# Attention stage of a hybrid decoder layer: later joins of first halves, later sample parts, and products with values ahead of the transposes

## The chip, the core and the metric

The kernel runs on one core of one Trainium2 chip. The metric is device time in microseconds (us) of one launch, median of several runs. A core has five engines with instruction streams of their own: TensorE (PE) multiplies matrices, VectorE (DVE) and ScalarE (ACT) do elementwise work and reductions, GpSimd (POOL) elementwise work, SyncE (SP) issues the transfers here. Streams meet at semaphores. PE writes its results to banks of PSUM, from which DVE and ACT read.

## What is computed

One layer for a prompt of 2048 rows and 8 samples of 8 rows, which share weights: a normalised, modulated input goes through one wide projection; branch A is sliding-window attention in three groups of 8 heads with strides 1, 4 and 16; branch B a gated recurrence; both are projected, gated, merged and added to the input. The part that the change touches is branch A:

```python
s = q @ k.T * scale - slope * dist          # per head, block of 128 queries: own and previous key block
m = max(s); p = exp(s - m); l = sum(p)
o = (p @ v) / l;  lse = m + log(l)
...
alpha = softmax over the 3 groups of lse     # head slot j of the three groups
o_a = sum over groups of alpha * o           # then times silu(z_A)
```

Samples do the same against a cache of earlier keys and values.

## The kernel before

Stages run one after the other: the input stage, `phase_weave` (projections and recurrence), `phase_mix` (attention), `phase_tail` (merge and output projection). The change is in `phase_mix`.

**Jobs and steps.** `JOBS` are the 12 combinations of 4 head pairs and 3 groups (2, 1, 0 in each pair); a job has 16 blocks of 128 queries, a step each, so N = 192. Steps of group 2 (and every fourth of group 1, the first of group 0) see one key block, those of the rest two; the text calls them light and full. Light steps fill steps 0 to 15, 48 to 63, 96 to 111 and 144 to 159.

**One block through the engines.** `score` (PE, L1482) multiplies queries with keys; `largest` (DVE, L1696) adds the distances and takes the minimum of the negated scores; `weights` (ACT, L1613) takes exponentials; `turn` (PE, L1490) transposes them; `copy_turned` (ACT, L1621) copies the transposes out of PSUM; `weigh` (PE, L1503) multiplies them with the values and a column of ones; `leave_sums` (DVE, L1703) moves the result to `o_out`, and SP stores it to `sums` in DRAM (L1392), four blocks at a time. At step n, PE runs `score(n)`, `turn(n-1)`, `weigh(n-2)`; ACT `weights(n)`, then `copy_turned(n-1)`; DVE `leave_sums(n-3)`, then `largest(n)`.

**Sample parts.** The samples' attention is cut into 4 groups (two samples each) of 13 parts, placed between steps by `at(i, k)`: parts 0 to 3 are scores (L1521, L1527), 4 to 7 transposes (L1539), 8 to 11 products with cached values (L1554), 12 selects the output (L1570). At a step that has a part, PE runs it behind `weigh`. The tables `S_PREPARE` (queries, DVE), `S_LARGEST`, `S_EXP`, `S_COPY`, `S_LOAD` (SP) and so on follow from `at`. SP loads the 32 stages of cached keys (L1402) and values (L1406) two ahead, each behind the part that frees its buffer; a stage is 2 MB but for the fourth of each four, which is smaller.

**Joins.** When a pair has its three groups, their rows are joined in two halves of 8 blocks. SP loads the rows from `sums` (L1425, 1.6 MB) and the gates (L1426); DVE takes the least maximum (`join_least`, L1756), ACT exponentials, DVE the weights (`join_weight`); POOL makes the weighted sums (DVE in the last pair); PE transposes each block (`join_turn`, L1590); DVE multiplies with the gate; SP stores. `start(jp, half)` and the tables `J_LOAD`, `J_LEAST`, `J_EXP`, `J_WEIGHT`, `J_SUM`, `J_TURN` place these. For the first halves of pairs 0 to 2, J_LOAD is at step 53, 101 or 149 and J_LEAST two steps later. Every table is read in a loop over n that each engine runs in order.

**Loads of a job.** At the fifth step of a job SP loads queries, keys, distances and values of the next (L1370 to L1380, 3.4 MB), behind the last use of the buffers, which is the end of the job before.

Of the kernel before, what the change touches and what calls it, by code (L numbers as in the profile page):

```python
# [21 lines left out]
PAIRS = 4  # L22
# [1225 lines left out]
def phase_mix(nc, t, dr):  # L1248
# [4 lines left out]
    N = len(JOBS) * BLK  # L1253
# [4 lines left out]


    SPAN, PARTS = 46, 13  # L1260
    at = lambda i, k: 4 + SPAN * i + k * SPAN // PARTS
    S_PE = {at(i, k): (i, k) for i in range(SB // 2) for k in range(PARTS)}
    S_PREPARE = {at(i, 0) - 2: i for i in range(SB // 2)}
    S_LARGEST = {at(i, c) + 1: (i, c) for i in range(SB // 2) for c in range(4)}
# [7 lines left out]

    start = lambda jp, half: BLK * (3 * jp + 3) + (5 + 20 * half if jp < PAIRS - 1 else 8 * half - 3)
    J_HALVES = [(jp, half) for jp in range(PAIRS) for half in range(2)]
    turn_at = lambda jp, half: start(jp, half) + (12 if jp < PAIRS - 1 else 6 + 2 * half)
    J_LOAD = {start(*x): x for x in J_HALVES}
    J_LEAST = {start(*x) + 2: x for x in J_HALVES}
    J_EXP = {start(*x) + 3: x for x in J_HALVES}
    J_WEIGHT = {start(*x) + 4: x for x in J_HALVES}
    J_SUM = {start(*x) + (7 if x == (PAIRS - 1, 1) else 5): x for x in J_HALVES}  # L1280
    S_LAST = [at(i, PARTS - 1) for i in range(SB // 2)]

    def turn_slot(jp, half, b):
# [12 lines left out]
    with ExitStack() as ctx:  # L1296
# [65 lines left out]
        with nc.Block() as block:  # L1362
# [107 lines left out]
            def _(pe):  # L1470
                def score(n):
                    a, i = divmod(n, BLK)
                    first = first_of(n)
                    if i == 0:
                        pe.wait_ge(q_in[a % 2], 16 * (a // 2 + 1))
                        pe.wait_ge(k_in[a % 2], 16 * (a // 2 + 1))
                    if n:
                        pe.wait_ge(max_done, 2 * n)
                    for h in range(2):
                        q = q_sb[a % 2][h * HD:(h + 1) * HD, i * P:(i + 1) * P]  # L1480
                        k = k_sb[a % 2][h * HD:(h + 1) * HD, (i - 1 + first) * P:(i + 1) * P]
                        pe.matmul(s_ps[h][:, first * P:], q, k, start=True, stop=True).then_inc(s_done, 1)  # L1482

                def turn(n):
                    pe.wait_ge(exp_done, 2 * n + 2)
                    if n >= 2:
                        pe.wait_ge(copy_done, n - 1)
                    for h in range(2):
                        for b in range(first_of(n), 2):
                            mm = pe.transpose(t_ps[n % 2][:, 2 * h + b, :], probs[n % 2][:, h, b * P:(b + 1) * P], t["ident"][:, :])  # L1490
                    mm.then_inc(t_done, 1)

                def weigh(n):
                    a, i = divmod(n, BLK)
                    first = first_of(n)
                    if i == 0:
                        pe.wait_ge(v_in[a % 2], 64 * (a // 2 + 1))
                    pe.wait_ge(copy_done, n + 1)
                    if n:
                        pe.wait_ge(o_done, n)  # L1500
                    for h in range(2):
                        for b in range(first, 2):
                            mm = pe.matmul(o_ps[:, h, :], probsT[n % 2][:, 2 * h + b, :], v_sb[a % 2][:, i + b - 1, h, :],  # L1503
                                           start=(b == first), stop=(b == 1))
                    mm.then_inc(pv_done, 1)
# [67 lines left out]
                def sample_part(i, k):  # L1573
                    if k < 4:
                        sample_scores(i, k)
                    elif k < 8:
                        sample_turn(i, k - 4)
                    elif k < 12:
                        sample_weigh(i, k - 8)
                    else:  # L1580
                        sample_out(i)

                def join_turn(jp, half, b):
                    nth = NTH[jp, half]
                    pe.wait_ge(sums, 5 * (nth + 1))
                    if nth or b:
                        pe.wait_ge(jx_done, HB * nth + b)
                    if samples_ahead(turn_slot(jp, half, b)):
                        pe.wait_ge(so_done, samples_ahead(turn_slot(jp, half, b)))
                    pe.transpose(jt_ps[:, :], joined[:, b].rearrange("p h d -> p (h d)"), t["ident"][:, :]).then_inc(jt_done, 1)  # L1590

                for n in range(END):
                    if n < N:
                        score(n)
                    if 1 <= n <= N:
                        turn(n - 1)
                    if 2 <= n <= N + 1:
                        weigh(n - 2)
                    if n in S_PE:
                        sample_part(*S_PE[n])  # L1600
                    if n in J_TURN:
                        join_turn(*J_TURN[n])

            @block.scalar
            def _(act):
# [24 lines left out]
                def sample_copy(i, r):  # L1630
                    act.wait_ge(st_done, 4 * i + r + 1)
                    if i and r == 0:
                        act.wait_ge(stage_done, 8 * i)
                    src = x_ps[:, :].rearrange("p (m q) -> p m q", q=P)
                    if r < 3:
                        act.copy(s_probsT[:, 4 * r:4 * r + 4, :], src[:, :, :]).then_inc(s_copy_done, 1)
                        return
                    act.copy(s_probsT[:, 12:13, :], src[:, 0:1, :])
                    act.copy(s_probsT[0:G * ST, KEYS, :], src[0:G * ST, 1, :]).then_inc(s_copy_done, 1)

                def join_weights(jp, half):
                    act.wait_ge(diff_done, NTH[jp, half] + 1)
                    act.activation(wgt[:, :, :, :], wgt[:, :, :, :], ACT.Exp).then_inc(e_done, 1)

                act.preload_act_table_set("natural_log_exp_and_others")
                for n in range(END):
# [6 lines left out]
                    if n in S_COPY:  # L1653
                        sample_copy(*S_COPY[n])
                    if n in J_EXP:
                        join_weights(*J_EXP[n])

# [24 lines left out]
            def _(dve):  # L1682
# [61 lines left out]
                def sample_leave(i):  # L1744
                    new = slice(2 * i * ST, 2 * (i + 1) * ST)
                    dve.wait_ge(ot_done, i + 1)
                    dve.wait_ge(zs_in, 16)
                    dve.tensor_tensor(o_s[:, :, new], ot_ps[:, :, :], z_s[:, :, new], ALU.mult).then_inc(so_done, 1)

                def join_least(jp, half):  # L1750
                    nth = NTH[jp, half]
                    dve.wait_ge(rows_in, 48 * (nth + 1))
                    if nth:
                        dve.wait_ge(sums, 5 * nth)
                    neg_max = rows[:, :, :, :, HD + 1]
                    dve.tensor_tensor(j_least[:, :, :], neg_max[:, 0], neg_max[:, 1], ALU.min).then_inc(small, 1)  # L1756
                    dve.wait_ge(small, 7 * nth + 1)
                    dve.tensor_tensor(j_least[:, :, :], j_least[:, :, :], neg_max[:, 2], ALU.min).then_inc(small, 1)
                    dve.wait_ge(small, 7 * nth + 2)
                    dve.tensor_tensor(wgt[:, :, :, :], j_least[:, :, :].unsqueeze(1).broadcast_to([P, G, HB, 2]), neg_max,  # L1760
                                      ALU.subtract).then_inc(diff_done, 1)
# [29 lines left out]
                for n in range(END):  # L1791
# [12 lines left out]
                    if n in S_OUT:  # L1804
                        sample_leave(S_OUT[n])
                    if n in J_LEAST:
                        join_least(*J_LEAST[n])
                    if n in J_WEIGHT:
                        join_weight(*J_WEIGHT[n])
                    if n in J_SUM and J_SUM[n][0] == PAIRS - 1:  # L1810
                        weighted_sums(dve, *J_SUM[n])
                    if n - 1 in J_TURN:
# [408 lines left out]
```

## Time and profile before

| | us |
|---|---|
| median of 3 runs (3141.14 to 3145.24) | 3144.12 |
| profiled execution, own time | 3146.13 |
| its span | 3144.3 |
| PE busy over the span | 2896.0 (92%) |
| DVE, ACT, POOL busy | 1322.7, 1077.5, 820.1 |
| granted clock of PE, mean of the span | 0.941 |

In the profile, PE is a matmul and PEld the load of its stationary operand; the granted clock is 1.00 at 2.4 GHz and 0.50 at 1.2 GHz. Ends of matmuls are modelled. An idle time is put down to the engine, line and tile that released it, as `<-DVE mix_o_out L1703`. SPq rows are SP's issues of transfers, with the time that SP took for them. The page cuts the span in 40 slices; the attention stage lies in slices 28 to 35, where PE's row falls to 5 to 9 tenths.

### The profile page before, as it was taken

Reading aid. Unit: us, or ns where it says so; the run is one execution under the profiler, and the core shown is the slowest. Engines: PE = TensorE matmul, PEld = TensorE weight load, DVE = VectorE, ACT = ScalarE, POOL = GpSimd, SP = SyncE. Lnnn points to the kernel's source line nnn. Section 1 sums busy time; section 2 is a strip of 40 time slices with the busy share of each in tenths; the row PEclk is TensorE's granted clock in tenths of the full one; section 3 lists DMA queues with packets and bytes.
Section 4 is the critical chain, followed back from the end, with each engine's and each line's share of the span. In section 5 each row is a group of like instructions: output and inputs, shape, how many; then the busy total and the mean of one; then the engine's idle time right before and its main releaser. Section 6 shows DMA issues by size and latency. Waiting matters only on the chain. (4 is left out here: it accounts for less than half of the span.)

```text
span 3144.3 us, 46944 instructions
## 1 busy us (share of the span) xinstructions
PE 2896.0 (92%) x17964; PEld 2598.6 (83%) x17964; DVE 1322.7 (42%) x3014; ACT 1077.5 (34%) x2109; POOL 820.1 (26%) x690
## 2 busy tenths in 40 slices
PE   7479999999999899999999999995979898579999
PEld 6468999888888799999999999994656666379999
DVE  2623234665444323233564655432434343433433
ACT  1233212444444434212444444432535444230110
POOL 0231223555422212223554542220011112040000
PEclk7589999999999999999999999997989797799999
DMA  6522432333332342323223332226676867363432
GB/s 189 198 93 87 125 94 73 103 98 104 102 105 86 113 169 85 121 75 95 88 89 115 94 107 94 82 90 236 232 259 209 278 233 238 103 208 113 123 122 88
DMA packets 341583, 417.89 MB, mean 133 GB/s; under 512 B 62705, under 2 KB 252401, under 8 KB 334705
## 3 DMA queue, kind: packets, MB, share of 16 engines
q1 hardware_dynamic: 334448, 406.23, 40.2%
q10 hardware_dynamic: 6912, 8.65, 0.8%
q8 instruction: 144, 2.36, 0.3%
q14 instruction: 79, 0.64, 0.1%
HBM read 284.11 MB, written 130.70 MB: 132 GB/s over the span
## 5 line engine op out<-in xcount | busy, mean ns | idle before, releaser
L680 PE MATMUL weave_bank<-h_high,weave_w_high 128*128 128x352 f32 (+2 forms) x2240 | 813.8, 363 | 45.0 <-POOL weave_w_low L921 31.0
L682 PE MATMUL weave_bank<-h_high,weave_w_low 128*128 128x352 f32 (+2 forms) x2240 | 793.7, 354 | 0.0
L681 PE MATMUL weave_bank<-h_low,weave_w_high 128*128 128x352 f32 (+2 forms) x2240 | 793.5, 354 | 0.0
L921 POOL TENSOR_TENSOR weave_w_low<-weave_w_raw,weave_w_high 128x512 fp32r<-128x512 f32 x288 | 380.2, 1332 | 797.6 <-ACT weave_w_high L817 795.7
L680 PEld LDWEIGHTS weave_bank<-h_high,weave_w_high 128*128 128x128 f32 x2240 | 425.6, 190 | 83.4 <-issue 46.8
L681 PEld LDWEIGHTS weave_bank<-h_low,weave_w_high 128*128 128x128 f32 x2240 | 426.0, 190 | 35.8 <-issue 2.9
L682 PEld LDWEIGHTS weave_bank<-h_high,weave_w_low 128*128 128x128 f32 x2240 | 425.0, 190 | 36.3
L692 PE MATMUL weave_bank<-weave_w_high,h_high 128*128 128x256 f32 x1088 | 311.6, 286 | 0.0
L693 PE MATMUL weave_bank<-weave_w_low,h_high 128*128 128x256 f32 x1088 | 307.9, 283 | 0.0
L694 PE MATMUL weave_bank<-weave_w_high,h_low 128*128 128x256 f32 x1088 | 307.9, 283 | 0.0
L1613 ACT ACTIVATE mix_probs<-mix_scores,mix_o_out 128x256 f32<-128x256 f32 (+1 forms) x384 | 156.6, 454 | 318.3 <-DVE mix_o_out L1696 306.4
L843 ACT ACTIVATE weave_out<-weave_out 128x352 f32<-128x352 f32 (+1 forms) x160 | 89.1, 557 | 480.5 <-DVE weave_out L1020 480.5
L933 POOL TENSOR_TENSOR weave_sq_low<-weave_sq,weave_sq_high 128x512 fp32r<-128x512 f32 (+2 forms) x120 | 138.3, 1152 | 366.1 <-DVE weave_sq_high L990 364.9
L1020 DVE TENSOR_SCALAR weave_out<-weave_bank 128x352 f32<-128x352 f32 (+1 forms) x160 | 95.6, 597 | 325.0 <-PE weave_bank L682 324.2
L1696 DVE CUSTOM_DVE_ANT_0 mix_scores<-mix_s_head,mix_dist 128x256 f32<-128x256 f32 (+1 forms) x384 | 126.9, 364 | 226.1 <-PE mix_s_head L1482 214.3
L1503 PE MATMUL mix_o<-mix_v,mix_probsT 128*128 128x65 f32 x1200 | 168.9, 281 | 47.8 <-DVE mix_o_out L1703 47.5
L693 PEld LDWEIGHTS weave_bank<-weave_w_low,h_high 128*128 128x128 f32 x1088 | 208.9, 192 | 0.6 <-issue 0.5
L692 PEld LDWEIGHTS weave_bank<-weave_w_high,h_high 128*128 128x128 f32 x1088 | 208.7, 192 | 0.6 <-issue 0.5
L694 PEld LDWEIGHTS weave_bank<-weave_w_high,h_low 128*128 128x128 f32 x1088 | 208.8, 192 | 0.0
L1503 PEld LDWEIGHTS mix_o<-mix_v,mix_probsT 128*128 128x128 f32 x1200 | 160.5, 204 | 52.5 <-issue 49.6
L817 ACT CAST weave_w_high<-weave_w_raw 128x512 fp32r<-128x512 f32 x288 | 167.9, 609 | 90.4 <-PE weave_bank L694 56.0
L871 ACT ACTIVATE weave_d<-weave_d 128x512 f32<-128x512 f32 (+1 forms) x144 | 84.6, 588 | 254.3 <-DVE weave_d L1091 240.0
(189 smaller groups left out, 4724.3 us busy)
## 6 DMA issues: line engine op xcount, KB each, us to landing
weave_w_raw<-in_w_qkv SPq DMA_DIRECT2D x144, 256.0 KB, 3.1
mix_kv<-in_kT_c SPq DMA_DIRECT2D x24, 1024.0 KB, 7.5
mix_kv<-in_v_c SPq DMA_DIRECT2D x24, 1024.0 KB, 7.0
tail_gates<-scratch_gates SPq DMA_DIRECT2D x48, 352.0 KB, 3.2
weave_w_raw<-in_w_b SPq DMA_DIRECT2D x64, 256.0 KB, 3.0
weave_w_raw<-in_w_g SPq DMA_DIRECT2D x64, 256.0 KB, 2.9
scratch_sums<-mix_o_out SPq DMA_DIRECT2D x48, 264.0 KB, 6.1
mix_rows<-scratch_sums SPq DMA_DIRECT2D x24, 528.0 KB, 6.9
```

Source lines behind the costliest of these rows:

```text
L680: pe.matmul(dst, w_high[:, i, k, :], h_high[:, k, tok], start=(k == 0), stop=False)
L681: pe.matmul(dst, w_high[:, i, k, :], h_low[:, k, tok], start=False, stop=False)
L682: mm = pe.matmul(dst, w_low[:, i, k, :], h_high[:, k, tok], start=False, stop=(k == KD - 1))
L692: pe.matmul(dst, h_high[:, k, lo:lo + P], w_high[:, i:i + 2, k, :], start=(k == 0), stop=False)
L693: pe.matmul(dst, h_high[:, k, lo:lo + P], w_low[:, i:i + 2, k, :], start=False, stop=False)
L694: mm = pe.matmul(dst, h_low[:, k, lo:lo + P], w_high[:, i:i + 2, k, :], start=False, stop=(k == KD - 1))
L817: act.copy(w_part(w_high, p), w_raw[p % RAW][:, :, :]).then_inc(w_high_done, 1)
L921: pool.tensor_tensor(w_part(w_low, p), w_raw[p % RAW][:, :, :], w_part(w_high, p), ALU.subtract).then_inc(w_low_done, 1)
L933: pool.tensor_tensor(sq_low[:, 0:w], sq[:, 0:w], sq_high[:, 0:w], ALU.subtract).then_inc(sq_low_done, 1)
L1503: mm = pe.matmul(o_ps[:, h, :], probsT[n % 2][:, 2 * h + b, :], v_sb[a % 2][:, i + b - 1, h, :], start=(b == first), stop=(b == 1))
L1613: act.activation(probs[n % 2][:, h, first * P:], scores[n % 2][:, h, first * P:], ACT.Exp, scale=-1.0, bias=o_out[a % 2][:, i, h * 66 + 65 ...
L1696: dve.tensor_tensor_reduce(scores[n % 2][:, h, first * P:], s_ps[h][:, first * P:], dist[a % 2][:, h, first * P:], 1.0, 3.0e38, ALU.add, A ...
```

## The change

`at` begins at 8 and not 4, so all sample parts and what hangs on them come four steps later. `later` puts the joins of first halves (not their loads) five steps back in pairs 0 to 2. On PE, `weigh(n - 2)` is issued ahead of `turn(n - 1)`. Two lines are added above, so line numbers behind them are larger by 2 in the changed kernel.

```diff
     SPAN, PARTS = 46, 13
-    at = lambda i, k: 4 + SPAN * i + k * SPAN // PARTS
+    at = lambda i, k: 8 + SPAN * i + k * SPAN // PARTS
...
-    turn_at = lambda jp, half: start(jp, half) + (12 if jp < PAIRS - 1 else 6 + 2 * half)
+
+    later = lambda jp, half: 5 if jp < PAIRS - 1 and half == 0 else 0
+    turn_at = lambda jp, half: start(jp, half) + later(jp, half) + (12 if jp < PAIRS - 1 else 6 + 2 * half)
     J_LOAD = {start(*x): x for x in J_HALVES}
-    J_LEAST = {start(*x) + 2: x for x in J_HALVES}
-    J_EXP = {start(*x) + 3: x for x in J_HALVES}
-    J_WEIGHT = {start(*x) + 4: x for x in J_HALVES}
-    J_SUM = {start(*x) + (7 if x == (PAIRS - 1, 1) else 5): x for x in J_HALVES}
+    J_LEAST = {start(*x) + later(*x) + 2: x for x in J_HALVES}
+    J_EXP = {start(*x) + later(*x) + 3: x for x in J_HALVES}
+    J_WEIGHT = {start(*x) + later(*x) + 4: x for x in J_HALVES}
+    J_SUM = {start(*x) + later(*x) + (7 if x == (PAIRS - 1, 1) else 5): x for x in J_HALVES}
...
                     if n < N:
                         score(n)
+                    if 2 <= n <= N + 1:
+                        weigh(n - 2)
                     if 1 <= n <= N:
                         turn(n - 1)
-                    if 2 <= n <= N + 1:
-                        weigh(n - 2)
```

What now stands where. PE, two full steps of group 0 (`mix_s_head` scores, `mix_t` transposes, `mix_o` products with values), before:

```order
L1482 MATMUL mix_s_head<-mix_kT,mix_qT 128x256 x2
L1490 MATMUL mix_t<-ident,mix_probs 128x128 x4
L1503 MATMUL mix_o<-mix_v,mix_probsT 128x65 x4
L1482 MATMUL mix_s_head<-mix_kT,mix_qT 128x256 x2
L1490 MATMUL mix_t<-ident,mix_probs 128x128 x4
L1503 MATMUL mix_o<-mix_v,mix_probsT 128x65 x4
```

And now:

```order
L1484 MATMUL mix_s_head<-mix_kT,mix_qT 128x256 x2
L1505 MATMUL mix_o<-mix_v,mix_probsT 128x65 x4
L1492 MATMUL mix_t<-ident,mix_probs 128x128 x4
L1484 MATMUL mix_s_head<-mix_kT,mix_qT 128x256 x2
L1505 MATMUL mix_o<-mix_v,mix_probsT 128x65 x4
L1492 MATMUL mix_t<-ident,mix_probs 128x128 x4
```

Products and transposes have changed places; between a transpose and the product that uses its copy stands one score.

SP around the first half of pair 0 (`mix_kv` sample keys, `mix_qT` to `mix_v` the next job, `mix_rows` the rows to be joined), before:

```order
L1402 DMA mix_kv_0<-in_kT_c 128x4x512 x2
L1370 DMA mix_qT<-scratch_qT 128x2048
L1371 DMA mix_kT<-scratch_kTo 128x2048
L1374 DMA mix_dist<-in_dist 128x512
L1380 DMA mix_v<-scratch_v_rows 128x4x130 x4
L1392 DMA scratch_sums<-mix_o_out 128x4x132
L1387 DMA out_v_p<-mix_v 128x2080
L1425 DMA mix_rows<-scratch_sums 128x8x132 x3
L1426 DMA mix_z<-scratch_zs 128x1024
L1402 DMA mix_kv_1<-in_kT_c 128x4x128 x2
```

And now:

```order
L1372 DMA mix_qT<-scratch_qT 128x2048
L1373 DMA mix_kT<-scratch_kTo 128x2048
L1376 DMA mix_dist<-in_dist 128x512
L1382 DMA mix_v<-scratch_v_rows 128x4x130 x4
L1394 DMA scratch_sums<-mix_o_out 128x4x132
L1389 DMA out_v_p<-mix_v 128x2080
L1427 DMA mix_rows<-scratch_sums 128x8x132 x3
L1428 DMA mix_z<-scratch_zs 128x1024
L1404 DMA mix_kv_0<-in_kT_c 128x4x512 x2
L1404 DMA mix_kv_1<-in_kT_c 128x4x128 x2
```

The keys that stood ahead of the next job's load and the rows stand behind them.

SP around the first half of pair 2, same tiles, before:

```order
L1402 DMA mix_kv_0<-in_kT_c 128x4x512 x2
L1392 DMA scratch_sums<-mix_o_out 128x4x132
L1431 DMA scratch_branch<-mix_j_out 128x1024
L1402 DMA mix_kv_1<-in_kT_c 128x4x128 x2
L1370 DMA mix_qT<-scratch_qT 128x2048
L1371 DMA mix_kT<-scratch_kTo 128x2048
L1374 DMA mix_dist<-in_dist 128x512
L1380 DMA mix_v<-scratch_v_rows 128x4x130 x4
L1392 DMA scratch_sums<-mix_o_out 128x4x132
L1387 DMA out_v_p<-mix_v 128x2080
L1425 DMA mix_rows<-scratch_sums 128x8x132 x3
L1426 DMA mix_z<-scratch_zs 128x1024
```

And now:

```order
L1433 DMA scratch_branch<-mix_j_out 128x1024
L1394 DMA scratch_sums<-mix_o_out 128x4x132
L1404 DMA mix_kv_0<-in_kT_c 128x4x512 x2
L1372 DMA mix_qT<-scratch_qT 128x2048
L1373 DMA mix_kT<-scratch_kTo 128x2048
L1376 DMA mix_dist<-in_dist 128x512
L1382 DMA mix_v<-scratch_v_rows 128x4x130 x4
L1394 DMA scratch_sums<-mix_o_out 128x4x132
L1389 DMA out_v_p<-mix_v 128x2080
L1427 DMA mix_rows<-scratch_sums 128x8x132 x3
L1428 DMA mix_z<-scratch_zs 128x1024
L1404 DMA mix_kv_1<-in_kT_c 128x4x128 x2
```

Here the large stage of keys (512 wide) has moved next to the load, still ahead of it, and the small one (128 wide) behind the rows.

## Rows read from the trace of the kernel before

**Rows 1.** Windows (us): length, busy of PE, PEld, DVE, ACT, POOL (count), PEclk, DMA share, GB/s.

```profile
2327.40:2336.00 8.60, 8.58 (x31) 4.19 (x31) 2.37 (x15) 2.04 (x7) 4.67 (x3) 0.60 0.25 70
2464.80:2491.40 26.60, 26.54 (x167) 22.49 (x167) 10.45 (x61) 11.91 (x34) 10.40 (x5) 0.50 0.70 262
2605.40:2635.20 29.80, 29.64 (x180) 24.38 (x180) 10.72 (x64) 13.21 (x37) 10.41 (x5) 0.51 0.69 251
2154.90:2748.20 593.30, 495.55 (x3392) 342.63 (x3392) 236.32 (x1170) 243.09 (x612) 62.49 (x30) 0.86 0.69 230
2300.00:2327.00 27.00, 10.60 (x70) 6.30 (x68) 5.28 (x32) 4.75 (x15) 0.00 (x0) 0.76 1.04 336
```

**Rows 2.** Waits of PE in 2295:2350, 2445:2480, 2580:2620: us, times, longest.

```profile
PE mix_o L1503 <- DVE mix_o_out L1703: 16.7, 1, 16.7
...
PE mix_o L1503 <- DVE mix_o_out L1703: 11.7, 1, 11.7
...
PE mix_o L1503 <- DVE mix_o_out L1703: 12.8, 1, 12.8
```

**Rows 3.** Timeline around the three joins: start, us, engine, line, operation [idle before].

```profile
2291.02 0.30 PEld L1482 LDWEIGHTS mix_s_head<-mix_kT,mix_qT 64*128 64x128 f32 x4
2300.96 0.62 SPq L1370 DMA_DIRECT2D mix_qT<-scratch_qT  x1
...
2326.38 0.19 DVE L1756 TENSOR_TENSOR mix_j_least<-mix_rows 128x16 f32<-128x16 f32 x1 [16.80 <-DMA mix_rows<-scratch_sums]
...
2463.82 0.19 DVE L1756 TENSOR_TENSOR mix_j_least<-mix_rows 128x16 f32<-128x16 f32 x1 [15.27 <-DMA mix_rows<-scratch_sums]
...
2573.03 0.30 PEld L1482 LDWEIGHTS mix_s_head<-mix_kT,mix_qT 64*128 64x128 f32 x4
2576.51 3.65 PE L1521 MATMUL mix_x<-mix_kv,mix_q_diag 128*64 128x512 f32 x16
2581.47 0.62 SPq L1370 DMA_DIRECT2D mix_qT<-scratch_qT  x1
...
2604.39 0.19 DVE L1756 TENSOR_TENSOR mix_j_least<-mix_rows 128x16 f32<-128x16 f32 x1 [12.87 <-DMA mix_rows<-scratch_sums]
```

**Rows 4.** Timeline of light steps, at full clock and, the last two rows, at half.

```profile
2444.61 0.30 PEld L1482 LDWEIGHTS mix_s_head<-mix_kT,mix_qT 64*128 64x128 f32 x4
...
2446.10 0.30 PEld L1482 LDWEIGHTS mix_s_head<-mix_kT,mix_qT 64*128 64x128 f32 x4
...
2446.30 0.35 ACT L1621 COPY mix_probsT<-mix_t 128x256 f32<-128x256 f32 x1
2446.53 0.44 PE L1490 MATMUL mix_t<-ident,mix_probs 128*128 128x128 f32 x2
2446.80 0.56 PE L1503 MATMUL mix_o<-mix_v,mix_probsT 128*128 128x65 f32 x4
2447.35 0.30 PEld L1482 LDWEIGHTS mix_s_head<-mix_kT,mix_qT 64*128 64x128 f32 x4
...
2476.54 0.51 PEld L1482 LDWEIGHTS mix_s_head<-mix_kT,mix_qT 64*128 64x128 f32 x4
2478.64 0.51 PEld L1482 LDWEIGHTS mix_s_head<-mix_kT,mix_qT 64*128 64x128 f32 x4
```

**Rows 5.** Wait of PE at the stage's start, 2150:2200.

```profile
PE mix_x L1521 <- DMA mix_kv<-in_kT_c: 12.8, 1, 12.8
```

**Rows 6.** Timeline of a full step at full clock, PE and PEld.

```profile
2281.92 0.30 PEld L1482 LDWEIGHTS mix_s_head<-mix_kT,mix_qT 64*128 64x128 f32 x4
2283.05 1.00 PE L1503 MATMUL mix_o<-mix_v,mix_probsT 128*128 128x65 f32 x8
2283.98 0.30 PEld L1482 LDWEIGHTS mix_s_head<-mix_kT,mix_qT 64*128 64x128 f32 x4
```

**Rows 7.** Timeline of the last block: its transposes and their copy.

```profile
2708.75 0.66 PE L1490 MATMUL mix_t<-ident,mix_probs 128*128 128x128 f32 x4 [0.23 <-ACT mix_probs L1613]
2709.45 0.58 ACT L1621 COPY mix_probsT<-mix_t 128x512 f32<-128x512 f32 x1 [0.28 <-PE mix_t L1490]
```

## Prediction

> **What bounds the kernel now.** I read the page first, to find the stage that the diff touches: attention, from 2154.9 to 2748.2 us, with TensorE (PE) busy for 495.55 of its 593.30 us at a mean granted clock of 0.86 [rows 1]. So 97.7 us are lost to waits, and more to a half clock. Then the waits. Three times PE stands for over 11 us before a product with values (L1503) that waits for VectorE (DVE): 16.7, 11.7 and 12.8 us, 41.2 together [rows 2]. The timeline names what DVE itself waits for each time: the first operation of a join (L1756) has waited 16.80, 15.27 and 12.87 us for the rows loaded from `sums` [rows 3]. DVE runs in order, so score minima and copies of later steps are stuck behind the join, and PE behind them. These waits cost twice. After each, PE is busy all the time but at half clock: 8.60 us at 0.60, 26.60 at 0.50, 29.80 at 0.51 [rows 1], which makes 6.9 + 26.6 + 29.2 = 62.7 us at 1.2 GHz. A light step (one key block, 128 columns) takes 2.10 us there, from 2476.54 to 2478.64, where two at full clock take 2447.35 - 2444.61 = 2.74, so 1.37 each [rows 4].
>
> **Term 1, start of the stage.** `at` goes from 4 to 8: sample parts, and what DVE, ScalarE (ACT) and SP do for them, come four steps later. Before, DVE holds PE up at step 2, where it prepares queries; at step 4 PE waits 12.8 us for the first sample keys [rows 5]. SP issues those keys without a gate, so they land when they did. In the new order, steps 4 to 7 run inside that wait. Once the part is through, step 9 starts where step 5 did: four light steps gained, 4 x 1.37 = 5.5 us. Bounds 0 and 8.4 (four at 2.10). **-5.5.**
>
> **Term 2, the three waits.** Both sides move: when DVE asks for the rows, and when they land. I count from the first step of the light job, which begins at 2291.02 in the first pair (step 48) and at 2573.03 in the third (step 144) [rows 3].
>
> DVE asked at landing minus wait: 2309.58 and 2591.52, in both 18.5 us after that start. Now it asks five steps later, 5 x 1.37 = 6.9. A long sample part keeps PE 3.65 us [rows 3]. In the first pair `sample_out` comes in besides (about 1 us, estimated from its 8 small products); in the second one long part and a `sample_out`; in the third one long part. So DVE asks 26.4 us after the start in the first pair, 29.1 in the third, and 6.9 + 3.65 + 1 = 11.6 later than before in the second.
>
> Landing, first pair: the load of the next job (L1370) began at 2300.96, right behind two transfers of sample keys of 1 MB each, and rows landed at 2326.38, 25.4 later [rows 3]. SP no longer waits for step 50's part ahead of that load, so it can go at the start of step 48, behind the previous transfer of sample values: 25.4, against 26.4. No wait for rows; but the keys of the part at step 61 now stand behind them. With the gates these are 2.5 MB; at the 336 GB/s of this stretch [rows 1] 7.4 us, so they land at 32.8, and PE gets there at 26.4 + 2 x 1.37 = 29.1: 3.7 us of a new wait. Second pair: asking 11.6 us later takes most of the 15.27, and SP's load no longer waits for the long part at step 96, 3.65 more: nothing left. The third pair goes the other way. Its load began at 2581.47 and rows landed 22.9 later, with 2 MB of keys sent well before. Now the keys gated by the part at step 146 stand directly ahead of the load. It starts after that part, at 1.85 (step 144, estimated between a light and a full step since its products are full ones) + 2 x 1.37 + 3.65 + 2 x 0.62 for SP's issue of the keys (as for 1 MB [rows 3]) = 9.5, and with 2 MB in front takes the first pair's 25.4: 34.9, against 29.1, so 5.8 us remain. Left over: 3.7 + 0 + 5.8 = 9.5. **-31.7.** Bounds: 0 (it all moves along) and -41.2.
>
> The Trainium skill (DMA: Bandwidth & Descriptors, Specifications) puts HBM's limit for one core at about 358 GB/s. The stretch's 336 [rows 1] agrees as a ceiling; by 358 the third landing would come 1.6 us sooner and the term be 1.6 us larger.
>
> **Term 3, clock.** 62.7 us at half clock would take 1.37/2.10 of it, saving 21.8. The wait that remains in the third pair may still drop it; no row shows what a wait of 6 us at full clock does. I leave half of that pair's 29.2 x 0.35 = 10.2 us unsaved. **-16.7.** Bounds 0 and -21.8.
>
> **Term 4, products ahead of transposes.** It speaks against the change. At step n PE now runs score(n), weigh(n-2), turn(n-1). weigh(n-2) needs copy_turned(n-2), which ACT runs behind the exponentials of n-1. Before, a whole step lay between a transpose and the product that uses its copy; now only score(n) does. So each step has the loop product, transposes, copy, next product, with PE idle for the part that a score does not fill. Full steps (two key blocks): 2283.98 - 2281.92 = 2.06 now, and PE is the limit. Products to next instruction 0.93 (2283.05 to 2283.98) [rows 6]; transposes 0.66; copy 0.04 after them (2709.45 against 2708.75 + 0.66), 0.58 long; this is the one place where ACT was free and waited for a transpose, 0.28 [rows 7]. With 0.08 for copy to product (estimate: the gaps between those rows are 0.04 to 0.15) that is 2.29 a step, +0.23. Light steps: 0.56 + 0.44 + 0.04 + 0.35 + 0.08 = 1.47 [rows 4], against 1.37 on average and 1.25 (2446.10 to 2447.35) where PE sets the pace: +0.10 to +0.22, I take +0.16.
>
> A sample part behind the transposes covers the copy, so the step after each of the 52 parts pays nothing: 140 of 192 pay. In proportion 79 of 108 full steps, 61 of 84 light ones: 79 x 0.23 + 61 x 0.16 = 18.2 + 9.8 = 28.0. Join transposes at a step's end cover some 0.12 us each (under half of the 0.27 from two transposes to the products behind them [rows 4]) in about 35 full steps: -4.2. **+23.8.** Bounds: 0, if the wait is filled, and 108 x 0.23 + 84 x 0.22 = +43. ACT's order lets me stay near the worked value.
>
> **At nothing:** the join's small DVE operations, its exponential and GpSimd's weighted sums move along, and the join transposes still come eight steps after the weights, as before, when PE waited at none of them in these pairs: those eight steps are the cover. If they didn't suffice, PE would wait at the first transpose, by what the sums are late. On SP the load of the second half keeps its place; the store of the first half's result comes five steps later, and what stands behind it is gated later anyway.
>
> **Sum.** -5.5 - 31.7 - 16.7 + 23.8 = -30.1. The profiled execution's 3146.13 (span 3144.3) becomes 3116.0; it lies 2.0 above the median of the runs, so 3144.12 becomes **3114**.
>
> **Rivals.** (a) Slower: DMA is the limit and the waits move with the join. For: the queues are full while DVE waits in the first pair, busy share 1.04 [rows 1], and PE without waits asks for the next data sooner. Against: after the first wait the share falls to 0.25 [rows 1], so there is room, and two loads start earlier. Then terms 2 and 3 are zero: -5.5 + 23.8 = +18.3, 3162. It decides if less than 18.3 of the 63 us in waits and clock comes back.
>
> (b) The wait of weigh costs nothing since PE works past it. For: in light steps PE already waits for exponentials, so a reordering could fill that. Against: in the trace products and transposes run in the program's order throughout. Term 4 is zero: 3144.1 - 53.9 = 3090. The Trainium skill (TensorE: Matmul & The Clock Gate, Architectural detail: the array is 16× 32×32, not 1× 128×128) says PE's queue is a partial reorder window that can pull weight loads ahead of running matmuls; no run here shows that it passes a load that waits.
>
> (c) The waits shrink but the clock stays low after shorter ones, since light steps never brought it back: in the second and third pair it stayed half for over 26 us of busy PE [rows 1]. Term 3 is zero: -13.4, 3131; with the copy loop at its upper bound, no change.
>
> **Numbers.** Forecast 0.62, (a) 0.15, (b) 0.08, (c) 0.15. A measurement tells 0.2%, 6.3 us, from no change. Faster: the forecast but for 0.03, (b), and 0.08 of (c), 0.75. Within 0.2%: 0.03 + 0.05 of (c) + 0.02 of (a) = 0.10. Slower: 0.13 of (a), 0.02 of (c): 0.15. The range leaves out most of (a) and the lower half of (b): 3092 (terms 2 and 3 in full, term 4 at two thirds: -5.5 - 63.0 + 15.9 = -52.6) to 3148 (terms 2 and 3 at half, term 4 half way to its bound: -5.5 - 24.2 + 33.4 = +3.7).
>
> **What would show it.** Right: DVE's wait for rows is gone in the first two pairs and about 6 us in the third; a few us of PE waiting for keys in the first; mean clock in the stage over 0.93; PE idle before L1505 put down to ACT's copies, in three steps of four; full steps at 2.3 us. Wrong: full steps still 2.06, or rows landing as late against the join as before, or clock at 0.5 in light steps without a wait before.

## The result and the profile after

The changed kernel takes 3164.57 us (median of 11 runs) against 3145.24 us (11 runs): a ratio of 1.006, 95% interval 1.004 to 1.008. Forecast were 30 us less; it came to 19 us more. The profiled execution took 3166.39 us (span 3164.6). Its last score ends at 2722.0 us, before at 2707.1, and the first product of the stage behind (`tail_ab`) starts at 2773.23 and not at 2756.90: 16 of the 20 us between the two profiled executions lie in the attention stage. Windows of the changed kernel, with the columns of [rows 1]: five stretches, then the stage.

```profile
2330.00:2352.50 22.50, 22.46 (x148) 17.58 (x148) 6.31 (x34) 9.17 (x21) 8.89 (x5) 0.54 0.89 321
2370.00:2392.50 22.50, 20.93 (x83) 13.94 (x83) 6.84 (x35) 8.27 (x20) 10.41 (x5) 0.54 0.10 37
2465.00:2500.00 35.00, 33.56 (x197) 25.68 (x197) 12.13 (x65) 14.95 (x37) 10.43 (x5) 0.56 0.79 275
2517.50:2530.00 12.50, 12.50 (x55) 8.37 (x56) 3.08 (x16) 4.27 (x9) 10.41 (x5) 0.59 0.18 65
2614.00:2656.00 42.00, 40.49 (x222) 31.71 (x222) 12.30 (x66) 16.56 (x38) 10.41 (x5) 0.51 0.79 266
2154.50:2764.00 609.50, 535.00 (x3392) 357.75 (x3392) 234.31 (x1170) 254.88 (x612) 62.48 (x30) 0.83 0.68 224
```

The stage's row stands against the fourth of [rows 1]: PE is busy for 535.0 us instead of 495.55 with the same 3392 matmuls, and its mean clock is 0.83, not 0.86. In the five stretches PE is busy nearly throughout, at half clock. Now the waits of PE, and DVE's for the rows, in the same kernel (us, times, longest), from 2310:2336, 2368:2373, 2464:2468, 2514:2519 and 2600:2618.

```profile
PE mix_o L1505 <- DVE mix_o_out L1705: 2.2, 2, 1.8
PE mix_x L1523 <- DMA mix_kv<-in_kT_c: 1.9, 1, 1.9
...
PE mix_turned L1592 <- issue: 1.6, 1, 1.6
...
PE mix_o L1505 <- DVE mix_o_out L1705: 1.4, 1, 1.4
...
PE mix_turned L1592 <- issue: 1.3, 1, 1.3
...
PE mix_x L1523 <- DMA mix_kv<-in_kT_c: 9.2, 1, 9.2
DVE mix_j_least L1758 <- DMA mix_rows<-scratch_sums: 6.4, 1, 6.4
```

The 41.2 us of [rows 2] are gone; DVE waits for rows only in the third pair, 6.4 us, and PE for keys 1.9 us in the first pair and 9.2 in the third. But the first four stretches at half clock begin right behind waits of only 1.3 to 1.8 us (a fifth of 1.3 us, at 2668, had no such stretch behind it). A sixth stretch, in light steps, has no wait over 0.3 us in the 20 us ahead of it:

```profile
2296.60:2303.40 6.80, 6.76 (x30) 4.05 (x31) 2.79 (x16) 2.93 (x9) 0.00 (x0) 0.50 1.10 351
```

Where the short waits come from, the timeline shows, here for the second:

```profile
2370.05 0.24 DVE L1768 TENSOR_TENSOR mix_den<-mix_wgt,mix_rows 128x48 f32<-128x48 f32 x1
...
2371.03 0.21 DVE L1776 TENSOR_TENSOR mix_wgt<-mix_wgt,mix_j_inv 128x48 f32<-128x48 f32 x1
2371.39 0.29 DVE L1788 TENSOR_TENSOR mix_j_out<-mix_turned,mix_z 128x128 f32<-128x128 f32 x1
...
2371.78 0.45 PE L1592 MATMUL mix_turned<-ident,mix_joined 128*128 128x128 f32 x1 [1.56 <-issue]
```

The first half's join transposes, five steps later, now run while DVE does the second half's weights (L1768 to L1776, 1.2 us), and these stand ahead of the gate (L1788) that the next transpose waits for. In the same way the two waits at L1505 stand behind small operations of the first half's join that share a step with a sample part's minimum. Last, full steps in the timeline, first at full and then at half clock.

```profile
2266.70 0.70 PE L1484 MATMUL mix_s_head<-mix_kT,mix_qT 64*128 64x256 f32 x4
2266.81 0.59 ACT L1623 COPY mix_probsT<-mix_t 128x512 f32<-128x512 f32 x1
2267.44 0.97 PEld L1505 LDWEIGHTS mix_o<-mix_v,mix_probsT 128*128 128x128 f32 x8 [0.44 <-ACT mix_probsT L1623]
...
2268.92 0.70 PE L1484 MATMUL mix_s_head<-mix_kT,mix_qT 64*128 64x256 f32 x4
...
2383.05 1.23 PE L1484 MATMUL mix_s_head<-mix_kT,mix_qT 64*128 64x256 f32 x4
2383.15 0.59 ACT L1623 COPY mix_probsT<-mix_t 128x512 f32<-128x512 f32 x1 [1.41 <-PE mix_t L1492]
2384.20 1.78 PEld L1505 LDWEIGHTS mix_o<-mix_v,mix_probsT 128*128 128x128 f32 x8 [0.65 <-ACT mix_probsT L1623]
...
2386.53 0.80 PE L1484 MATMUL mix_s_head<-mix_kT,mix_qT 64*128 64x256 f32 x2
```

At full clock the copy ends at 2267.40 and the product's load starts 0.04 us later: the loop of term 4. The step lasts 2.22 us against 2.06 [rows 6]; so it does behind a plain step. Behind a step with a sample part or a join's transpose, whose work covers the copy, it lasts 2.11 at full clock. So 0.05 us come with the order and 0.11 with the wait for the copy. At half clock a step lasts 3.48, and there the copy is done 0.46 before the product: the loop no longer binds.

### The profile page after: what moved, and what is told of

It reads as the page before. It is cut to its first block and busy times, and to the rows that moved or that the text cites. A ratio compares the mean times of both kernels' runs of the same rounds, so it can differ in the third digit from the quotient of the medians.

```text
span 3164.6 us, 46944 instructions
## 1 busy us (share of the span) xinstructions
PE 2942.1 (93%) x17964; PEld 2621.4 (83%) x17964; DVE 1325.2 (42%) x3014; ACT 1089.7 (34%) x2109; POOL 820.9 (26%) x690
## 5 line engine op out<-in xcount | busy, mean ns | idle before, releaser
L1505 PEld LDWEIGHTS mix_o<-mix_v,mix_probsT 128*128 128x128 f32 x1200 | 170.8, 215 | 79.7 <-ACT mix_probsT L1623 54.9
L1505 PE MATMUL mix_o<-mix_v,mix_probsT 128*128 128x65 f32 x1200 | 198.6, 309 | 19.9 <-ACT mix_probsT L1623 9.0
```

## The experiments

Three numbers of each profiled execution are used. **Clock**: the mean granted clock from 2200 to 2640 us, a row of the windows. **Half-clock work**: over windows of 2.5 us from the first score to 20 us before the end of the last, PE's busy time times (1 - clock)/0.5. A **plain full step** is one without a sample part or a join's transpose, from its scores to the next, at full clock; a common length is given (with 2.22, steps behind a part last 2.11, or 2.17 where the needless transpose described below is added). Ratios are to the kernel before, run on the same chip.

| kernel | median us | ratio (95%) | clock | half-clock work | plain full step |
|---|---|---|---|---|---|
| before | 3145.24 | 1 | 0.89 | 79 | 2.06 |
| changed | 3164.57 | 1.006 (1.004-1.008) | 0.86 | 148 | 2.22 |
| e_no_swap | 3128.53 | 0.9938 (0.9915-0.9961) | 0.92 | 81 | 2.06 |
| e_swap_only | 3206.24 | 1.0188 (1.0163-1.0214) | 0.84 | 174 | 2.22 |
| e_join_only | 3127.35 | 0.9932 (0.9911-0.9953) | | 92 | 2.06 |
| e_parts_only | 3136.39 | 0.9965 (0.9949-0.9982) | | 55 | 2.06 |
| e_lag | 3154.37 | 1.0007 (0.9988-1.0026) | 0.85 | 160 | 2.11 |
| e_fill | 3150.13 | 0.9996 (0.9979-1.0013) | 0.92 | 86 | 2.22 |
| e_gap | 3183.63 | 1.0114 (1.0093-1.0135) | 0.89 | 136 | 2.40 |
| e_lag_fill | 3140.91 | 0.9981 (0.9969-0.9992) | 0.94 | 63 | 2.17 |
| e_first_fill | 3129.98 | 0.9939 (0.9922-0.9957) | 0.93 | 72 | 2.17 |
| e_gap_fill | 3163.74 | 1.0044 (1.0029-1.0059) | 0.93 | 79 | 2.40 |
| e_swap_fill | 3168.76 | 1.0057 (1.0043-1.0070) | 0.90 | 73 | 2.22 |
| e_turn2 | 3130.01 | 0.9941 (0.9920-0.9962) | | 79 | 2.06 |
| e_rows2 | 3120.57 | 0.9903 (0.9881-0.9926) | | 79 | 2.06 |
| e_best | 3144.23 | 0.9976 (0.9957-0.9995) | | 95 | 2.06 |
| e_best2 | 3099.65 | 0.9833 (0.9818-0.9849) | 0.97 | 51 | 2.06 |

### The change in parts

e_no_swap, the changed kernel with the two calls in their old order:

```diff
-                    if 2 <= n <= N + 1:
-                        weigh(n - 2)
                     if 1 <= n <= N:
                         turn(n - 1)
+                    if 2 <= n <= N + 1:
+                        weigh(n - 2)
```

> The changed kernel with the transposes put back ahead of the products; the later joins and the later sample parts stay. Theory A (the swap leaves PE a gap of 0.2 to 0.3 us in nearly every step, and these gaps are what lets the granted clock fall to half in stretches with no long wait): the half-clock stretches of the changed kernel at 2340, 2370 to 2395, 2467 to 2497 and 2619 to 2656 us are gone, half clock stands only behind what is left of the long waits, and the terms for the start, the waits and the clock come in nearly whole: 3144 - 5.5 - 25 - 17 = about 3097 us, 3090 to 3110. Theory B (the clock falls because of the later sample parts and joins and the waits that they leave, not because of the swap): the half-clock stretches stay and only the loop's 24 us come back: 3164 - 24 = about 3140 us, 3132 to 3148.

e_swap_only, the kernel before with the opposite edit:

```diff
+                    if 2 <= n <= N + 1:
+                        weigh(n - 2)
                     if 1 <= n <= N:
                         turn(n - 1)
-                    if 2 <= n <= N + 1:
-                        weigh(n - 2)
```

> The kernel before with only the swap (products ahead of transposes); joins and sample parts where they were. Theory A: the loop costs 24 us, and half-clock stretches appear in steps without a long wait, as in the changed kernel, for some 25 to 45 us more; the three long waits stay: 3144 + 24 + 25 to 45 = 3190 to 3215 us. Theory B: the loop's cost alone, with half clock only behind the three long waits as before: 3144 + 24 = about 3168 us, 3160 to 3180.

The swap costs 59 us on the kernel before and 36 us on the later joins and parts, more than its loop, and half-clock work about doubles with it both times. That is theory A. But e_no_swap missed A's 3097 by 31 us (and lies 4 us under B's range): taking the long waits away did not take half clock away (81 against 79). Three windows of e_no_swap show where it stays: behind a wait of 1.3 us, behind one of 1.6, and in light steps at the second join, where no wait over 0.9 us stands ahead.

```profile
2327.00:2349.50 22.50, 22.50 (x150) 18.66 (x150) 6.65 (x38) 9.51 (x23) 9.91 (x5) 0.54 0.93 330
2368.60:2374.00 5.40, 5.37 (x30) 3.88 (x30) 2.18 (x11) 1.75 (x4) 4.77 (x3) 0.68 0.41 149
2454.90:2471.90 17.00, 16.85 (x118) 13.77 (x119) 5.62 (x30) 6.27 (x16) 10.42 (x5) 0.50 0.92 360
```

The other two parts, alone; e_join_only is e_no_swap with

```diff
-    at = lambda i, k: 8 + SPAN * i + k * SPAN // PARTS
+    at = lambda i, k: 4 + SPAN * i + k * SPAN // PARTS
```

> The kernel before with only the later joins of the first halves; transposes first, sample parts where they were. Both theories: the three waits for the rows shrink from 41 us to about 6 to 15 us, with keys still late in the third pair. Theory A: the clock is lost only behind the waits that are left: 3144 - 26 to 35 - 10 to 17 = 3095 to 3110 us. Theory B: the later joins or the waits that move bring their own half-clock stretches: 3120 to 3140 us.

e_parts_only is the kernel before with

```diff
-    at = lambda i, k: 4 + SPAN * i + k * SPAN // PARTS
+    at = lambda i, k: 8 + SPAN * i + k * SPAN // PARTS
```

> The kernel before with only the sample parts four steps later; transposes first, joins where they were. Both theories: the wait for the first keys shrinks from 18 to about 7.5 us, the three waits for rows stay: 3144 - 5.5 = about 3139 us by theory A, 3134 to 3144, with half clock only behind those waits. Theory B, if the parts' new places next to the joins are what lets the clock fall: 3150 us or more.

Each is faster by itself, by 0.68% and 0.35%; together they give 0.62%, no more than the joins alone. Theory B's 3120 to 3140 held for the joins, and theory A's 3134 to 3144 for the parts.

### Is it idle time in each step?

e_lag takes the products one step later (with a third buffer for the copied transposes, and `leave_sums` a step later on DVE; those lines are left out here), e_fill puts a needless transpose where PE waits for the copy, both on the changed kernel:

```diff
-                    if 2 <= n <= N + 1:
-                        weigh(n - 2)
+                    if 3 <= n <= N + 2:
+                        weigh(n - 3)
```

> The changed kernel, its order on PE kept (scores, products, transposes), but the products of step n-3 instead of n-2, with a third buffer for the copied transposes: no step waits for its copy any more. Theory A1 (the wait for the copy in each step is what costs, by itself and by the clock that falls and stays low with it): the idle time of PE's weight loads before the products behind the copy (54.9 us on the changed kernel's page) falls below 10 us, half clock in steps with work falls from about 148 to about 80 us as in the kernel with the transposes first, and the time is that kernel's: 3128 us, 3118 to 3138. Theory A2 (the order of the three on PE does it, with or without the wait): it stays within 3150 to 3175 us.

```diff
+                FILL = 1
...
+                    if 2 <= n <= N:
+                        if n >= 3:
+                            pe.wait_ge(copy_done, n - 2)
+                        for x in range(FILL):
+                            pe.transpose(t_ps[(n - 1) % 2][:, x, :], t["ident"][:, :], t["ident"][:, :])
                     if 2 <= n <= N + 1:
                         weigh(n - 2)
```

> The changed kernel with one more transpose in each step, of the identity into a bank that is overwritten before it is read, put between the scores and the products, where PE waits for the copy: 0.21 us of needless PE work in each of 191 steps. If it lay beside nothing it would cost 191 x 0.21 = 40 us: 3164 + 40 = 3205. Theory A1 in its strong form (idle PE time is what the clock answers to): the work fits into the gap, PE is idle no longer, half clock in steps with work falls from 148 to 80 us, which gives back about 35 us, and the time is 3125 to 3150 us. Theory A3 (the clock answers to the long and middle waits alone, and half clock merely lasts longer because each step is longer): 3165 to 3205 us.

With 191 more transposes the kernel is 14 us faster: steps last 2.22 us as without them (2.17 instead of 2.11 behind a step with a part), and half-clock work falls from 148 to 86. e_lag falls where theory A2 put it: full steps last 2.11, the copy is hardly waited for (from 2200 to 2640 us PE waits 0.4 us for it, in the changed kernel 6.6), and yet half-clock work stays at 160. So there the order lost the clock without the wait for the copy. PE still waits 17 times for DVE's `mix_o_out`, 9.4 us in all (e_no_swap: 5 times, 3.4 us); whether that does it, no run tells. To ask whether a gap is enough without the order, the same pair was made of other kernels. e_gap is e_no_swap with a wait, its order unchanged; e_gap_fill puts the transpose into that wait:

```diff
+                    if 2 <= n < N:
+                        pe.wait_ge(max_done, 2 * n + 1)
                     if 2 <= n <= N + 1:
                         weigh(n - 2)
```

> The kernel with the transposes first and the later joins and parts (3128.5 us), with one wait added in each step and no order changed: before its products PE also waits for DVE's first minimum of this step's scores, which by that kernel's timeline comes 0.1 to 0.2 us after the transposes are through. So it has the changed kernel's step length without its order. Theory G (a short gap in every step makes half clock last): half clock in steps with work rises from 81 to 120 us or more, and the time is 3128 + 20 for the steps + 15 for the clock = 3163 us, 3152 to 3175. Theory O (it is the order scores, products, transposes, not the gap): half clock stays at 70 to 95 us and only the steps get longer: 3128 + 20 = 3148 us, 3138 to 3151.

```diff
                     if 2 <= n < N:
+                        pe.wait_ge(copy_done, n - 1)
+                        pe.transpose(t_ps[n % 2][:, 0, :], t["ident"][:, :], t["ident"][:, :])
                         pe.wait_ge(max_done, 2 * n + 1)
```

> The gap run (3183.6 us, half clock in steps with work 136 us, full steps 2.40 us) with the needless transpose put into its gap: the wait for DVE's first minimum stays, PE works while it waits. If idle time in each step is what makes half clock last: half clock falls to 60 to 95 us, steps stay at 2.40 us, and the time is 3183 - 20 = 3163 us, 3152 to 3172. If the longer step alone does it: half clock stays above 120 us and the time at 3175 us or more.

e_lag_fill, e_first_fill and e_swap_fill have e_fill's lines ahead of the products of e_lag, ahead of the transposes of e_no_swap, and ahead of the products of e_swap_only:

```diff
+                        pe.transpose(t_ps[(n - 1) % 2][:, 0, :], t["ident"][:, :], t["ident"][:, :])
```

> The kernel with products one more step behind (3154 us, half clock in steps with work 160 us although full steps at full clock last 2.11 us) with the needless transpose in each step of the fill run. Theory O with activity (with products behind the scores the engine is too lightly used to get its clock back, and any added work brings it back): half clock falls to 70 to 100 us, time 3125 to 3150 us. If the fill run got its clock back only by closing the wait for the copy: no wait is closed here, the transposes cost their time, and it is 3160 to 3190 us.

> The kernel with the transposes first and the later joins and parts (3128.5 us), with the needless transpose in each step between the scores and the transposes. There is little half clock left to win (81 us, some 40 of it in the first 35 us of the stage): at 0.1 to 0.21 us in each of 191 steps it costs 19 to 40 us, less 0 to 10 us for clock: 3138 to 3168 us. If an added transpose is worth more in clock than it costs in time whatever the order, it would be 3128 us or less.

> The kernel before with the swap alone (3206 us, half clock in steps with work 174 us) with the needless transpose between scores and products. The three long waits for the rows stay. If work in the gap brings the clock back whatever else stands in the stage: half clock falls to 80 to 110 us and the time to 3165 to 3185 us. If half clock behind the long waits lasts because of the waits: 3195 to 3220 us.

The windows from 2200 to 2640 us, first of the changed kernel and of e_fill:

```profile
2200.00:2640.00 440.00, 408.21 (x2664) 274.81 (x2660) 165.85 (x872) 198.09 (x474) 52.07 (x25) 0.86 0.73 244
```

```profile
2200.00:2640.00 440.00, 414.60 (x2905) 281.73 (x2904) 173.17 (x904) 206.75 (x495) 52.13 (x25) 0.92 0.75 247
```

then of e_gap and of e_gap_fill:

```profile
2200.00:2640.00 440.00, 413.97 (x2622) 270.06 (x2620) 165.62 (x854) 183.38 (x461) 41.64 (x20) 0.89 0.69 233
```

```profile
2200.00:2640.00 440.00, 422.13 (x2843) 284.96 (x2844) 172.67 (x891) 193.25 (x485) 52.08 (x25) 0.93 0.73 246
```

In each pair the filled kernel gets through more steps in the same 440 us (DVE's counts: 872 to 904, 854 to 891), at a higher clock. e_gap's wait came out longer than meant (0.34 us a step, 2.40), so its time is above the range given; but with the order unchanged half-clock work rose from 81 to 136, and with the gap filled it was 79 again at the same 2.40. The times of e_gap_fill, e_lag_fill and e_swap_fill lie where the first theory of each put them. In four kernels the transposes gave 14, 37, 13 and 20 us (changed, swap only, lag, gap; by the ratios 20, 41, 8 and 22, where the intervals of the lag pair just overlap). So a gap in each step is enough to lose the clock with the order unchanged, a longer step alone is not, and added work brought the clock back in all four. That the work has to lie in a gap is not shown. In e_lag there was hardly a wait for the copy to fill. In e_first_fill there was no gap; its full steps last 2.17 and not 2.06, some 12 us over the 108 of them, but its time is only 1.5 us above e_no_swap, under the 3138 to 3168 that were expected. The intervals, 6 to 7 us either way, leave open whether the work won some clock there too. Why e_lag loses the clock without the wait for the copy is not shown either.

### What is left in the joins

e_turn2 on e_no_swap; e_rows2 on e_turn2; then e_best and e_best2, each on e_rows2:

```diff
-    turn_at = lambda jp, half: start(jp, half) + later(jp, half) + (12 if jp < PAIRS - 1 else 6 + 2 * half)
+    turn_at = lambda jp, half: start(jp, half) + later(jp, half) + ((12 if half else 14) if jp < PAIRS - 1 else 6 + 2 * half)
```

> The kernel with the later joins and sample parts and the transposes first, and the join's transposes of the first halves two steps later. There three waits of 1.4 to 1.6 us stand before the first of these transposes, and a stretch at half clock began right behind one of them. If waits of this size let the clock fall: the three waits go (4 us), and half clock behind them too (some 6 us of time): 3128.5 - 10 = 3118 us, 3110 to 3124. If they are harmless: 3124 to 3130 us.

```diff
-    later = lambda jp, half: 5 if jp < PAIRS - 1 and half == 0 else 0
+    later = lambda jp, half: 7 if jp < PAIRS - 1 and half == 0 else 0
-    J_LOAD = {start(*x): x for x in J_HALVES}
+    J_LOAD = {start(*x) + (2 if later(*x) else 0): x for x in J_HALVES}
```

> As the run before it, and the rows of the first halves are asked for two steps later, so that the keys of the part in between stand ahead of them in the queue, and their joins come seven steps later instead of five. If the waits of PE for these keys (5.3 and 10.2 us with the transposes first) are only a matter of the queue's order: both shrink to under 2 us, no new wait of DVE for the rows above 3 us, and with the clock behind them 15 to 25 us are won: 3128.5 - 10 - 20 = 3100 us, 3092 to 3110. If the transfers are the limit there and a wait only changes places: within 6 us of the run before it, with 8 us or more of waits for rows.

```diff
-((12 if half else 14) if jp < PAIRS - 1 else 6 + 2 * half)
+(((17 if jp < 2 else 12) if half else 16) if jp < PAIRS - 1 else 6 + 2 * half)
```

> The run with the rows asked for two steps later (3120.6 us), and the join's transposes two more steps later for the first halves and five for the second halves of the first two pairs. There PE waited 5.9, 4.3 and 2.8 us for the weighted sums before the first transpose of each first half, with half clock behind. If two steps (4 us) later take most of that: 3120 - 8 - 5 = 3107 us, 3098 to 3115. If the sums are late because the rows are and the wait moves on: within 5 us of 3120.

```diff
-    later = lambda jp, half: 7 if jp < PAIRS - 1 and half == 0 else 0
+    later = lambda jp, half: ((4, 4, 2)[jp] if half else 7) if jp < PAIRS - 1 else 0
...
-    J_LOAD = {start(*x) + (2 if later(*x) else 0): x for x in J_HALVES}
+    J_LOAD = {start(*x) + (2 if later(*x) == 7 else 0): x for x in J_HALVES}
```

> The run with the first halves' rows asked for two steps later (3120.6 us), and the joins of the second halves four steps later in the first two pairs and two in the third. In that run DVE waited for the second halves' rows, and the join's transposes of PE, which wait for DVE's gates, stood 5.9, 4.3 and 2.8 us. If lateness of the second halves' joins takes these waits: 3120 - 10 - 5 = 3105 us, 3098 to 3113. If transfers are the limit and the wait only moves: 3117 to 3126 us.

The profile of e_best2 was taken in a second run of the same kernel:

> The same kernel as the run with the later second halves (3099.7 us), for a profile that can be read. If the waits went: the three waits of 5.9, 4.3 and 2.8 us before the join's transposes are under 1.5 us each, DVE waits less than 6 us in all for rows between 2200 and 2680 us (18.4 before), and half clock in steps with work is 50 to 75 us. If they moved: a wait above 3 us stands somewhere else in that stretch besides the keys'.

e_turn2 won nothing: of three waits of 1.4 to 1.6 us two stayed and one became 4.5, as DVE then stood for the second half's rows (4.38 us) ahead of the gate. e_rows2 won 8 us over e_no_swap where 28 were expected; what stopped it shows in PE's waits from 2200 to 2675 us:

```profile
PE mix_turned L1592 <- issue: 15.1, 8, 5.9
PE mix_x L1523 <- DMA mix_kv<-in_kT_c: 5.3, 3, 4.0
```

The keys' waits fell (4.0 us at most and not 10.2, though not under the 2 us expected), but the join's transposes wait up to 5.9 us: their gates are DVE's, and DVE stands before the second half's join for its rows (5.90 us until 2350.26). e_best moved only the transposes, DVE still stood for rows (11.2 us in all), and the wait went to the products (4.8 us at L1505): a miss. That says why nothing was won, not why it is 24 us slower than e_rows2. Up to 2640 us the two have much the same waits and half clock; then e_best waits 3.2 us for POOL's weighted sums, and all steps from there to the last score run at half clock, where those of e_rows2 have 1.00 (e_best, then e_rows2):

```profile
2658.00:2702.00 44.00, 43.21 (x174) 31.42 (x175) 12.30 (x56) 12.46 (x27) 0.73 (x1) 0.50 0.24 74
2655.00:2678.50 23.50, 23.02 (x172) 16.96 (x170) 12.10 (x55) 12.43 (x27) 0.00 (x0) 1.00 0.37 103
```

This order has no gap in each step, so a gap is not needed either for half clock to last. e_best2 moved the second halves' joins instead, and PE's waits from 2200 to 2655 us are

```profile
PE mix_turned L1592 <- issue: 8.6, 12, 1.4
PE mix_x L1523 <- DMA mix_kv<-in_kT_c: 5.5, 2, 5.1
```

No wait of DVE for rows is left in that stretch, half-clock work is 51 us, and 3099.65 us beats both kernels: 1.67% under the kernel before.

## Why the prediction was wrong

- **Term 1** (-5.5): right in kind, and too small. PE's wait for the first sample keys fell from 12.8 [rows 5] to 7.5 us, and the wait at step 2 (5.1 us before), which the term names but does not count, is gone too. e_parts_only measures 0.35%, 0.18 to 0.51%, so 6 to 16 us.
- **Term 2** (-31.7): right for the waits that it counted. 9.5 us were to be left; 1.9 + 9.2 = 11.1 are. DVE's 6.4 us for rows in the third pair were forecast as 5.8; that the keys of the small sample part stand behind those rows there, and hold PE longer than the rows, was not. Nor were the five short waits, 7.4 us in all. The 336 GB/s of [rows 1] that it took for the transfers were no ceiling: the same trace has 419 GB/s from 2254 to 2264 us.
- **Term 3** (-16.7): this is the step that failed. It took half clock as a price of the three long waits, gone with them, and no term gave the swap a price in clock. e_no_swap has those waits gone and the order of before, and 81 us of half-clock work against 79: nothing came back. With the swap it is 148, and the time another 20 us longer (term 4). [Rows 1] showed what follows a wait of 11 us and more; I left what follows a short one for the third pair only, though the trace had no row on it. Waits of 1.3 to 1.8 us were enough in the changed kernel, and 17 us at half clock in e_no_swap came without even that. Rival (c), a clock that stays low after shorter waits, had this, with too small a chance and too small a price: it kept the half clock of before, where the swap raised it to 148.
- **Term 4** (+23.8): right for the loop. With the clock mostly level (86 against 81), e_fill over e_no_swap gives 0.9996 - 0.9938, 18 us, and e_swap_fill over the kernel before 0.57%, 18 us; both hold what the needless transposes cost besides. Full steps last 2.22, not 2.29, and 2.11, not 2.06, where a part covers the copy. What it left out is the swap's price in clock: 1.006 - 0.9996 is 0.6%, 20 us, and on the kernel before 1.0188 - 1.0057 is 1.3%, 41 us.
- **The sum**, in ratios: terms 1 to 3 gave -0.62%, -19.5 us, where -53.9 stood; the loop +18, the swap's clock +20: +19. Of the 34 us missing in terms 1 to 3, 16.7 are term 3. Some 12 are waits: with the order of before, e_no_swap keeps 16.2 us of waits for keys and 5.7 of short ones, where 9.5 were to be left. The rest lies within its interval of 7 us either way.
- **At nothing**: the joins' small operations were said to move along at no cost. But only the first halves moved: their transposes ran into the second halves' weights on DVE, and with both parts and joins later, joins and a part's minimum fell into one step. That is where the short waits come from.
- **Rival (a)** gave 3162, nearly the time that came, by a mechanism that did not: the waits did not move along, 41.2 us went to 11; that the time came out near it is luck. **Rival (b)**, products that cost nothing, fell with the 2.22 us steps. Of the signs, the stage's mean clock was to be over 0.93 and is 0.83, and "clock at 0.5 in light steps without a wait before" did come, from 2296.6 us; the other stretches had a wait before, but four of them a short one.

## What to carry to other kernels

A reordering that makes PE wait 0.1 to 0.3 us in most steps can have two prices, the step's and the clock's, and the second was as large as the first here. To see the second, put needless work into the gap: the clock's price is at least what the time loses by that. Taking the wait away by a longer lag did not save it (e_lag), so a new order is to be measured even where its waits are gone. And a wait that is taken away gives back its half clock only if no short wait takes its place, so look for what is next late before counting it.

## What the runs showed of the hardware

TensorE's clock went to half behind waits of 1.3 to 1.8 us in the changed kernel, with a gap in most steps, for 10 to 30 us of nearly unbroken work each time (the rows above), while in e_no_swap waits of 1.3 to 1.6 us were followed by 21, 3 and, twice, no us of it. It also went to half without such a wait (7 us in the changed kernel, 17 in e_no_swap), and in e_best, which has no gap in each step, it stayed there for 44 us of which PE was busy for 43.2. A needless transpose in each of 191 steps made four kernels faster by 13 to 37 us. The Trainium skill (TensorE: Matmul & The Clock Gate, A second HAM failure mode: psum-queue depth-cycling) tells of a kernel whose short idle times between groups of matmuls made the clock swing between its two levels; the pairs of runs agree (half-clock work 136 against 79 us in e_gap and e_gap_fill), and it is the rule that the prediction should have weighed against the swap.
